# Two transformer blocks with a 32-expert layer: another order in which the experts are taken

## The reference

```
def moe_ffn(h, w_router, b_router, w_exp_in, b_exp_in, w_exp_out, b_exp_out):
    t = h.reshape(-1, D)                                  # 256 tokens x 1024
    logits = (t @ w_router + b_router)                    # 32 experts
    top_val, top_idx = lax.top_k(logits, TOP_K)           # TOP_K = 4
    gate_w = jax.nn.softmax(top_val, axis=-1)
    ...
        hb = xb @ w_exp_in[e] + b_exp_in[e]               # 1024 -> 2048
        g = jnp.minimum(hb[:, :D_FF_2], SWIGLU_LIMIT)
        u = jnp.clip(hb[:, D_FF_2:], -SWIGLU_LIMIT, SWIGLU_LIMIT)
        a = g * jax.nn.sigmoid(SWIGLU_ALPHA * g) * (u + 1.0)
        return a @ w_exp_out[e] + b_exp_out[e]            # 1024 -> 1024
    ...
    y = jnp.einsum('nk,nkd->nd', gate_w, y_slot)
```

```
56 19 27 28  7 33 75  6 18 16 29 77  3 17 14 58 40 19 31 40 20 43 72  2 16  3 50 35 28 45 17 80
```

## Time and profile before

| | |
|---|---|
| median of 3 runs | 1488.91 us (1488.56 to 1490.25) |
| the profiled execution's own time | 1488.56 us |
| its span in the profile | 1486.7 us |
| TensorE busy | 1329.8 us (89% of the span) |
| first turn of the experts starts at | 547.4 us |
| bytes moved | 494.37 MB, mean 333 GB/s |
| mean granted TensorE clock | 0.982 |

### The profile page before, as it was taken

The page is one execution under the profiler, slowest core; times in us unless marked ns, Lnnn a source line. Parts: engine busy times, 40 slices in busy tenths (PEclk is TensorE's granted clock), DMA queues, the critical chain, the costliest instruction groups (busy, mean ns, idle before and its releaser), DMA issues.

```text
span 1486.7 us, 25548 instructions
## 1 busy us (share of the span) xinstructions
PE 1329.8 (89%) x9369; PEld 799.9 (54%) x9370; DVE 449.2 (30%) x910; ACT 360.2 (24%) x691; POOL 139.3 (9%) x65
## 2 busy tenths in 40 slices
PE   7999999999999999777989888998889978998885
PEld 6455999987889864333433433343343433343332
DVE  1326688745543881101111111111011101110112
ACT  1234666545666621001000100010010001000101
POOL 0000112104776400000000000000000000000000
PEclk9999999999999999999999999999999999999998
DMA  9442366855444489999999999999999999999996
GB/s 344 146 138 60 113 176 190 315 189 189 150 170 151 159 331 424 424 424 426 427 426 425 426 426 426 426 419 427 425 425 428 427 424 427 427 427 425 426 427 266
DMA packets 113494, 494.37 MB, mean 333 GB/s; under 512 B 7617, under 2 KB 55089, under 8 KB 80465
## 3 DMA queue, kind: packets, MB, share of 16 engines
q1 hardware_dynamic: 111971, 491.50, 82.4%
q10 hardware_dynamic: 1486, 2.34, 0.5%
HBM read 492.76 MB, written 1.06 MB: 332 GB/s over the span
## 4 chain that ended last, share of the span: by engine, by line
PE 60%; DMA 30%; issue 3%; DVE 3%; ACT 2%; SPq 0%; DVEq 0%; ACTq 0%
DMA big_mem<-in_w_exp_in 28%; PE ps L985 15%; PE ps L1027 7%; PE ps L703 5%; PE ps L705 5%; PE ps L704 5%; PE ps L531 4%; PE ps L968 3%; PE ps L675 2%; DMA big_mem<-in_w_exp_out 2%; PE ps L727 1%; PE ps L729 1%; PE ps L728 1%; PE ps L1050 1%; PE ps L520 1%
## 5 line engine op out<-in xcount | busy, mean ns | idle before, releaser
L985 PE MATMUL ps<-big_mem,ring_mem 128*32 128x512 f32 (+1 forms) x2304 | 368.2, 617 | 52.9 <-DMA big_mem<-in_w_exp_in 52.9
L985 PEld LDWEIGHTS ps<-big_mem,ring_mem 128*32 128x32 f32 (+1 forms) x2304 | 111.2, 122 | 286.3 <-issue 195.1
L1027 PE MATMUL ps<-big_mem,x 128*32 128x256 f32 (+1 forms) x1888 | 184.7, 434 | 5.0 <-ACT x L1598 3.3
L703 PE MATMUL ps<-hT_hi,w_hi 128*128 128x256 f32 x600 | 171.1, 285 | 1.3 <-DVE hT_lo L1685 1.3
L705 PE MATMUL ps<-hT_hi,w_lo 128*128 128x256 f32 x600 | 169.7, 283 | 0.0
L704 PE MATMUL ps<-hT_lo,w_hi 128*128 128x256 f32 x600 | 169.7, 283 | 0.0
L968 PEld LDWEIGHTS ps<-ring_mem,h 128*128 128x128 f32 x1024 | 132.2, 198 | 61.1 <-issue 61.1
L968 PE MATMUL ps<-ring_mem,h 128*128 128x96 f32 x1024 | 149.5, 290 | 0.0
L2177 DVE TENSOR_SCALAR ring_mem<-ps 128x256 f32<-128x256 f32 (+1 forms) x36 | 18.7, 520 | 404.3 <-PE ps L985 404.3
L1585 ACT ACTIVATE ring_mem<-ring_mem 128x256 f32<-128x256 f32 (+1 forms) x36 | 17.8, 493 | 468.7 <-DVE ring_mem L2177 468.7
L1027 PEld LDWEIGHTS ps<-big_mem,x 128*32 128x32 f32 (+1 forms) x1888 | 71.7, 116 | 104.3 <-issue 67.3
(11 more groups left out here) (349 smaller groups left out, 1499.4 us busy)
## 6 DMA issues: line engine op xcount, KB each, us to landing
big_mem<-in_w_exp_in SPq DMA_DIRECT2D x128, 2048.0 KB, 22.4
big_mem<-in_w_exp_out SPq DMA_DIRECT2D x128, 1024.0 KB, 21.5
ring_mem<-in_w_in SPq DMA_DIRECT2D x15, 2048.0 KB, 8.1
ring_mem<-in_w_up SPq DMA_DIRECT2D x44, 512.0 KB, 4.9
ring_mem<-in_w_down SPq DMA_DIRECT2D x5, 2048.0 KB, 8.8
ring_mem<-in_w_out SPq DMA_DIRECT2D x4, 2048.0 KB, 8.7
ring_mem<-in_w_branch_a SPq DMA_DIRECT2D x1, 2048.0 KB, 7.5
ring_mem<-in_w_branch_b SPq DMA_DIRECT2D x1, 2048.0 KB, 7.3
```

Source lines behind the costliest of these rows:

```text
L703: mm(out, hi, x_hi, start=start, stop=False)
L985: last = mm(out, stationary, weights[:, f, w * q:w * (q + 1)] if m > XS else weights[:, :, w * q:w * (q + 1)], start=start, stop=stop)
L1027: last = mm(ps[m * q:m * (q + 1), 4 + at // XS, 0:w], aT[:, k % n, k // n, :], wout[:, k, w * q:w * (q + 1)], start=(k == 0), stop=(k == K ...
```

## The change

One line of the table changes: the ranks at places 4 to 31.

```
-    stay[:, RANKS + 4:RANKS + E] = 12 * np.arange(1, E - 3)[None, :] % (E - 3) - 1
+    stay[:, RANKS + 4:RANKS + E] = 23 * (np.arange(E - 4)[None, :] + 26) % (E - 4)
```

## The result

| | before | after |
|---|---|---|
| median | 1489.58 us (1488.56 to 1490.74, 4 runs) | 1515.49 us (1514.63 to 1517.99, 4 runs) |
| the profiled execution's own time | 1488.56 us | 1515.6 us |
| its span | 1486.7 us | 1513.7 us |

The ratio is 1.0176, with a 95% interval of 1.0158 to 1.0194: the change costs 25.9 us. The forecast was 1512, within 1503 to 1521.

What follows compares the result with a forecast made beforehand. The prediction took weight transfers at 425 GB/s as the bound after the first expert. Late requests at four wide turns, 2.6 + 2.6 + 9.0 + 9.1 = 23.3 us, on 1488.6 plus 0.3 for the median gave 1512 us, range 1503 to 1521.

Steps and rivals of the forecast that it cites:

- four holes: Behind the wide turns at 6, 11, 17 and 28: empty DMA of about 9, 3, 9 and 3 us.
- the rival of the slow pairs: Places 11 and 28 may lose 1.6 us more each, 6 and 17 none: 1515 us; 0.15 together with stall twice.
- The reserve of 66.0 us: Latest request time after TensorE gets the last `win` pair of the turn before a wide one, without DMA loss.
- Places 11 and 28, 2.6 each: Wide turns with one middle turn ahead: 68.6 against 66.0 us, over by 2.6 each, bounds 1.8 and 4.2.
- the extra wait of 0.8 us: Before a wide turn behind a middle one: wait for ScalarE, taken as 0.8 us between 0 and 1.4.
- Place 17, 9.1: Wide turn behind middle turns 15 and 16 and `bias_out`: 104.6 against 95.5 us, over by 9.1.
- Place 6, 9.0: Wide turn behind middle turns 4 and 5, with the 5.5 us stall: 104.5 against 95.5 us, over by 9.0.
- The stall: TensorE idle 5.44 us after place 4, once, kept there; rival without it 1507 us, 0.22 together with small holes absorbed.
- The tail unchanged: End of the kernel: same narrow last turn, span still ending 15.1 us behind the last `wout` pair.
- The rule taken strictly, the stall twice: Rival: stall before place 5 and again at place 7, 5.5 us more, 1518 us; 0.15 together with slow pairs.
- Absorption: Rival: the queue holds at least 9 us more reserve at the wide turns, so no change, 1489 us; chance 0.06.
- a rate that hangs on the sequence: Rival, faster: weight rate depends on which experts follow each other, 428 against 425 GB/s, 1483 to 1487 us; chance 0.02.

Runs made afterwards that it cites:

- b_bias13: Kernel before with `bias_out` moved to follow the wide turn at place 13, order untouched: 1493.68 us, ratio 1.0026.
- b_bias14: Kernel before with `bias_out` moved to follow the narrow turn at place 14, order untouched: 1489.96 us, ratio 1.0004.
- a_swap5_30: Changed kernel with the experts of places 5 and 30 exchanged, so a narrow turn stands between 4 and 6: 1505.38 us, ratio 1.0092.

## Why the prediction was right

The mechanism held: four holes, at the places named, and the full rate outside them. The sum was too small, 23.3 us where the profiled execution lost 26.9, and it came this close partly by luck: places 11 and 28 came out 0.8 too large each, which hid some of the 3.9 that place 6 was too small by. The median, 1515.5, is also the figure of the rival of the slow pairs, 1515. A slower TensorE did come, but at places 6 and 17 and not at 11 and 28, where that rival had it.

- *The DMA is the bound although TensorE shows 89%.* Shown: TensorE's instructions are the same in both kernels and in b_bias13 and b_bias14, and the time follows the holes in the rate.
- *The reserve of 66.0 us.* Shown at both sides of its edge, by the landing times and by moving 5.2 us of work across it.
- *Places 11 and 28, 2.6 each.* They cost 1.8. The term that was too large is the extra wait of 0.8 us before a wide turn: 874.14 - 854.28, last pair to start, and 1387.44 - 1367.58 are both 19.9, where I had 20.5. A wide turn behind a middle one doesn't wait for ScalarE at all; it was behind narrow turns that it did. The lower bound, 1.8, was the value.
- *Place 17, 9.1.* It cost 9.5, from two errors of opposite sign: no extra waits (1.2 less), and the second product of place 15 took 8.78 us instead of 7.09 (1.7 more: from 1003.72 to 1025.09 are 21.4 us against 19.7). That the term is within 0.4 is luck.
- *Place 6, 9.0.* It cost 12.9, and this is the term that was mis-sized. The stall came where I had put it and as long, 5.44 us. But I counted place 5 as a middle turn at full speed, 30.4 + 0.8 us, and it took 724.75 - 689.50 = 35.3. Its first product took 16.50 us, not 13.95, and its second 8.78, not 7.09. The trace of before had the sign of it, which the prediction didn't read: behind the same stall, the first product of a narrow turn took 9.65 us, against 7.04 (at 964.68) where place 14 had its weights there and no stall. The clock rows of the changed kernel are below.

```profile
690.35 9.65 PE L985 MATMUL ps<-big_mem,ring_mem 128*32 128x512 f32 x64
```

- *The tail unchanged.* 1.2 us off: the last `win` pair took 3.54 us instead of 1.92, 1.6 more, and the last `wout` pairs were then no longer waited for.
- *Rivals.* The stall did not move or come twice: it stood before place 5 with a middle follower (5.44) as with a narrow one (5.44 before, 5.51 in a_swap5_30), and place 7 shows 0.31. So it doesn't hang on what comes behind. Every order here has its first middle turn of the loop at place 4, so no run tells the width from the place; but the first narrow turn of the loop, place 1, has the like behind it. The start of place 2 after the change, and the queue that the profile calls `instruction` between 680 and 695 us (packets, MB, share):

```profile
603.66 0.62 PE L985 MATMUL ps<-ring_mem 128*32 128x512 bf16 x4 [7.39 <-issue]
...
q8 instruction: 2, 0.03, 0.8%
```

One of the two packets moved at 685 to 686 us, inside the stall (684.1 to 689.5), and two more at 596 to 600, inside the one before place 2. Every run has two between 680 and 695 us and none from 695 to 1480, though each turn takes its branches. So the stalls come together with loads of code that happen once; whose code the packets carry the profile doesn't say, and no run takes them away. The Trainium skill, in "Runtime: NRT & Kernel Launch", "Instruction fetch mechanics", has a taken branch to a page outside the window of fetched ones wait for a fetch: that fits the first visits, and no run here shows it on any later one. The rule taken strictly, the stall twice, is refuted. Absorption and a rate that hangs on the sequence are refuted.

The granted clock in two stretches of the changed kernel, first product of place 5 and second product of place 15; the clock is the third number from the end:

```profile
689.50:707.00 17.50, 17.50 (x70) 6.81 (x70) 0.11 (x1) 0.00 (x0) 0.00 (x0) 0.83 1.02 427
...
1012.90:1021.70 8.80, 8.80 (x33) 2.64 (x34) 0.00 (x0) 0.00 (x0) 0.00 (x0) 0.81 1.00 425
```

A mean of 0.83 says that the engine had the lower of its levels, 1.2 GHz instead of 2.4, for a third of the time. In the first case it had stood still for 5.44 us just before. In the second it had had the short waits of places 14 and 15 for transfers. This slowness was forecast for places 11 and 28 as a bound of 1.6 and struck at 6 and 17, which I had called free of it. Nor does a wait by itself foretell a slow pair, as the prediction read it: the pairs at 900.78 and 1461.70 before waited the same 2.97 and 2.98 us and took 3.40 and 1.92. I ran nothing that changes the clock alone, so its share is read from rows, not shown by an experiment.

## What to carry to other kernels

Where one buffer is refilled piece by piece behind the engine that reads it, a stall of that engine costs nothing as long as its next request still goes out before the last one in flight has landed, here 2.9 us before; work out that moment from the trace (the landing time of a lone transfer is the sign that it has come), and add up what stands between two of the engine's own waits for data. The order of uneven work then matters even though its sum doesn't: put the short pieces ahead of and behind the longest ones, and extra work right behind the request that decides, not in front of it. Once the transfers never run dry, more reserve gains nothing.

## What the runs showed of the hardware that was not expected

- A TensorE that has stood still is slower afterwards: after 5.44 us of standing still its next product took 16.50 us instead of 13.95, and the second product of the same turn 8.78 instead of 7.09, 23 us after the stall had ended.
- In the page's 40 slices a hole is only as visible as its share of a slice: the 1.8 us holes read 405 GB/s beside 426. At place 13 before, the landing times give 0.1 us, and the slice reads 419, which would be 0.6 us; the prediction's 424 to 428 GB/s passed over this slice.
- While the queue runs dry, a 1 MiB pair lands 4.8 to 4.9 us after its issue (place 6 and 17 of the changed kernel, with at most one other pair on its way) and a lone 2 MiB pair 7.6 to 7.8 us, so 2.3 to 2.9 us come on top of the 2.5 and 4.9 us that they take in a full queue (a twelfth and a sixth of 29.5).
- In all twelve kernels profiled, the `instruction` queue moved its last packets between 690 and 695 us, and from 700 us to 1480 TensorE never again stood still for more than 1.0 us without a releaser.
